# Three narrow products become one wide and one narrow; the work behind a feature-major job is moved and spread

## The reference, cut to what matters

```
# projection of the second block; xbc are 3072 of its 8224 columns
z, xbc, dt_raw, q, k, v = split(rmsnorm(h) @ w_in)
xbc = silu(causal_depthwise_conv(xbc, 4 taps) + conv_b)

# feed-forward part; w_up is 2048 x 11264, w_down 5632 x 2048
u = rmsnorm(h) @ w_up
u = causal_depthwise_conv(u, 3 taps) + ffn_conv_b
g_ff, u_ff = split(u)
h = h + (silu(g_ff) * u_ff) @ w_down
```

## Time and profile before

| | |
|---|---|
| median of three runs | 2368.04 us (2367.92 to 2368.23) |
| the profiled execution | 2368.59 us |
| its span, first to last instruction | 2366.8 us |
| instructions | 33302 |
| TensorE busy | 2253.2 us, 95% |
| VectorE busy | 1397.2 us, 59% |
| ScalarE busy | 989.5 us, 42% |
| mean granted TensorE clock | 0.981 |

### The profile page before, as it was taken

The page is one execution under the profiler, slowest core; times in us unless marked ns, Lnnn a source line. Parts: engine busy times, 40 slices in busy tenths (PEclk is TensorE's granted clock), DMA queues, the critical chain, the costliest instruction groups (busy, mean ns, idle before and its releaser), DMA issues.

```text
span 2366.8 us, 33302 instructions
## 1 busy us (share of the span) xinstructions
PE 2253.2 (95%) x13134; PEld 1927.9 (81%) x13134; DVE 1397.2 (59%) x1955; ACT 989.5 (42%) x1413; POOL 110.8 (5%) x106
## 2 busy tenths in 40 slices
PE   5899999998799899999989999999999999999998
PEld 1387888996568788998759888899999999788877
DVE  1357565634745577676566544667767776544465
ACT  1333232334544444444456544444444443344453
POOL 1000000002300021000000000000000000000000
PEclk8999999999899999999989999999999999999999
DMA  9975565543025466556400466556565665666554
GB/s 367 348 217 167 186 213 169 152 128 93 1 71 187 138 187 192 175 183 199 142 1 1 147 202 195 149 174 186 178 194 169 185 184 165 205 194 192 194 165 164
DMA packets 209084, 399.86 MB, mean 169 GB/s; under 512 B 15257, under 2 KB 23965, under 8 KB 208012
## 3 DMA queue, kind: packets, MB, share of 16 engines
q1 hardware_dynamic: 205520, 386.71, 51.9%
q0 software_dynamic: 2160, 7.20, 1.3%
q10 hardware_dynamic: 1292, 4.41, 0.5%
HBM read 395.25 MB, written 3.01 MB: 168 GB/s over the span
## 4 chain that ended last, share of the span: by engine, by line
PE 86%; DVE 6%; DMA 4%; ACT 2%; issue 1%; POOL 1%; SPq 0%; DVEq 0%; ACTq 0%
PE bank L1765 51%; PE bank L1776 27%; DMA ada_ring<-in_w_ada 4%; PE bank L1878 1%; PE bank L2046 1%; PE bank L1939 1%; PE bank L1861 1%; PE bank L1928 1%; PE bank L2059 1%; DVE wlo L1079 1%; PE bank L1870 0%; PE bank L1930 0%; POOL st L570 0%; PE bank L1905 0%; ACT kt L677 0%
## 5 line engine op out<-in xcount | busy, mean ns | idle before, releaser
L1079 DVE TENSOR_TENSOR wlo<-raw,whi 128x1024 fp32r<-128x1024 f32 (+2 forms) x649 | 773.5, 1204 | 584.7 <-ACT whi L670 570.3
L670 ACT ACTIVATE whi<-raw 128x1024 fp32r<-128x1024 f32 (+2 forms) x649 | 669.6, 1045 | 858.8 <-PE bank L1765 413.2
L1765 PE MATMUL bank<-whi,xl 128*128 128x512 f32 (+2 forms) x1904 | 734.0, 386 | 20.1 <-DVE wlo L1079 10.0
L1765 PE MATMUL bank<-whi,xh 128*128 128x512 f32 (+2 forms) x1904 | 728.4, 383 | 0.0
L1765 PE MATMUL bank<-wlo,xh 128*128 128x512 f32 (+2 forms) x1904 | 728.2, 382 | 0.0
L1776 PE MATMUL bank<-xl,whi 128*128 128x256 f32 x1792 | 507.9, 283 | 0.3 <-DVE xl L1128 0.3
L1776 PE MATMUL bank<-xh,wlo 128*128 128x256 f32 x1792 | 507.3, 283 | 0.0
L1776 PE MATMUL bank<-xh,whi 128*128 128x256 f32 x1792 | 507.2, 283 | 0.0
L1765 PEld LDWEIGHTS bank<-whi,xl 128*128 128x128 f32 x1904 | 359.1, 189 | 93.9 <-DVE wlo L1079 12.5
L1765 PEld LDWEIGHTS bank<-wlo,xh 128*128 128x128 f32 x1904 | 359.2, 189 | 68.7
L1765 PEld LDWEIGHTS bank<-whi,xh 128*128 128x128 f32 x1904 | 359.3, 189 | 65.7
(11 more groups left out here) (310 smaller groups left out, 1570.5 us busy)
## 6 DMA issues: line engine op xcount, KB each, us to landing
raw<-in_w_in SPq DMA_DIRECT2D x216, 512.0 KB, 4.4
raw<-in_w_up SPq DMA_DIRECT2D x176, 512.0 KB, 3.7
raw<-in_w_out SPq DMA_DIRECT2D x96, 512.0 KB, 4.6
raw<-in_w_down SPq DMA_DIRECT2D x88, 512.0 KB, 4.8
ada_ring<-in_w_ada SPq DMA_DIRECT2D x64, 512.0 KB, 11.6
gate_w<-in_w_ada SPq DMA_DIRECT2D x32, 512.0 KB, 3.9
raw<-in_w_ple_gate SPq DMA_DIRECT2D x32, 512.0 KB, 4.9
raw<-in_w_in SPq DMA_DIRECT2D x16, 384.0 KB, 3.3
```

The lines of the kernel that those rows point to most:

```text
L670: nc.scalar.activation(whi[:, slot, 0:size], raw[:, slot, 0:size], ACT.Copy).then_inc(hi_ready, 1)
L1079: tt_(wlo[:, slot, 0:size], raw[:, slot, 0:size], whi[:, slot, 0:size].bitcast(F32), ALU.subtract).then_inc(lo_ready, 1)
L1765: ins = mm(b4[tt][:, 0:width], x[:, o:o + P], w, start=k == 0 and i == 0, stop=k == last and i == 2)
```

## The change

`XH` and `XL` become the two halves of one tensor `XHL`. In `feature_major` a matmul of `whi` with 512 moving columns (256 of `XH`, then 256 of `XL`) and a matmul of `wlo` with the 256 columns of `XH` take the place of the three of 256 columns. The product is now in two halves of a bank, columns 0 to 255 (`whi` by `XH`) and 256 to 511 (the two others). So after each feature-major job ScalarE copies the upper half to SBUF and VectorE adds the lower half to it; only then are the banks free.

The taps then read SBUF. In the F jobs the first tap goes to ScalarE (slot 4), and VectorE has one tap a slot (5, 6, 7), tanh and silu follow in slots 9 and 10. In the `w_up` loop the copy and the addition come in slots 1 and 9, and all parts behind them one slot later. The last up job's parts are spread over the splits of the down tiles 2 to 8.

```diff
-        XH = at("xh", 12288, [P, 15360], FR)
-        XL = at("xl", 27648, [P, 15360], FR)
+        XHL = at("xhl", 12288, [P, 2, 15360], FR)
+        XH, XL = XHL[:, 0, :], XHL[:, 1, :]
+        UX = at("up_x", 51032, [P, 4, 256])
...
# TensorE, feature_major
-                        for i, (w, x) in enumerate(((whi, XL), (whi, XH), (wlo, XH))):
-                            ins = mm(b4[f][:, 0:256], w[:, slot, o:o + P], x[:, k * 256:(k + 1) * 256],
-                                     start=k == 0 and i == 0, stop=k == last and i == 2)
+                        mm(b4[f][:, :].rearrange("p (s n) -> p s n", s=2), whi[:, slot, o:o + P],
+                           XHL[:, :, k * 256:(k + 1) * 256], start=k == 0, stop=False)
+                        ins = mm(b4[f][:, 256:512], wlo[:, slot, o:o + P], XH[:, k * 256:(k + 1) * 256],
+                                 start=False, stop=k == last)
...
# ScalarE, F jobs
-                        ins = copy(XBC[:, (c - 2048) // P + i, :], b[i][:, 0:256])
-                    ins.then_inc(evac, 1)
+                        ins = copy(XBC[:, (c - 2048) // P + i, :], b[i][:, 256:512])
+                    ins.then_inc(low_copied, 1)
...
+                if kind == "F" and back == 4:
+                    act.wait_ge(evac, j + 1)
+                    if q >= 2:
+                        act.wait_ge(cv_used, q - 1)
+                    for i in range(4):
+                        k = 4 * q + i
+                        ins = nc.scalar.activation(CV[:, q % 2, i, :], XBC[:, k, :], ACT.Identity,
+                                                   scale=COLS[:, 200 + k:201 + k], bias=COLS[:, 80 + k:81 + k])
+                    ins.then_inc(tap0, 1)
-                if kind == "F" and back == 6:
+                if kind == "F" and back == 9:
...
# ScalarE, w_up jobs
+            def low_half(b4, used):
+                act.wait_ge(tile_used, used)
+                for f in range(4):
+                    ins = copy(UX[:, f, :], b4[f][:, 256:512])
+                ins.then_inc(low_copied, 1)
...
                 for k in range(16):
                     n = N_UP + 16 + k
                     hi(i * 16 + n, n % RING, 1024, i * 64 + 16 * (n // RING + 1))
-                    if k == 7:
+                    if k == 1:
+                        act.wait_ge(g_ready, i + 1)
+                        low_half(UB, i * 16 + (N_UP + 16))
+                    if k == 8:
                         act.wait_ge(ff_ready, i + 1)
...
+                    if k == 9:
+                        low_half(GB, i * 16 + (N_UP + 24))
-                    if k == 14:
+                    if k == 15:
...
-            for n in range(N_DN, N_DN + 4):
+            for n in range(N_DN, N_DN + 9):
                 split(n)
+                if n == N_DN + 1:
+                    low_half(UB, N_DN)
...
# VectorE, F jobs
-                if back in (3, 5):
...
+                if back == 3:
+                    dve.wait_ge(low_copied, q + 1)
+                    for i in range(4):
+                        x = XBC[:, 4 * q + i, :]
+                        ins = tt_(x, banks_of(j)[i][:, 0:256], x, ALU.add)
+                    own(ins)
+                    dve.sem_inc(evac, 1)
+                if back in (5, 6, 7):
+                    tap = back - 4
...
+                        ins = stt(y[:, tap:256], x[:, 0:256 - tap], wt, y[:, tap:256], ALU.mult, ALU.add)
...
# VectorE, w_up jobs
+            def whole(b4, count):
+                dve.wait_ge(low_copied, count)
+                for f in range(4):
+                    ins = tt_(UX[:, f, :], b4[f][:, 0:256], UX[:, f, :], ALU.add)
+                own(ins)
+                dve.sem_inc(evac, 1)
...
-                    if 1 <= k <= 6:
-                        after_up(i, i * 16 + (N_UP + 16), UB, k - 1)
+                    if 1 <= k <= 7:
+                        after_up(i, k - 2)
                     if k == 8:
                         low_product(i, i * 1024 + 4096)
-                    if 9 <= k <= 12:
-                        after_gate(i + 1, i * 16 + (N_UP + 24), GB, k - 9)
+                    if 9 <= k <= 13:
+                        after_gate(i + 1, k - 10)
             split(N_DN)
+            split(N_DN + 1)
+            after_up(10, -1)
             for part in range(6):
-                after_up(10, N_DN, UB, part)
-                if part in (1, 3, 4):
-                    split(N_DN + 1 + (1, 3, 4).index(part))
+                split(N_DN + 2 + part)
+                after_up(10, part)
+            split(N_DN + 8)
             low_product(10, 14336)
```

More of the change, by code:

```diff
@@ L677, in copy, with phase @@
                 return nc.scalar.activation(dst, src, ACT.Copy)
-            def phase(first, end, copy_out, later=None, moving=None):
-                for n in range(first + 2, end + 2):
+            def phase(first, end, copy_out, later=None, moving=None, begin=None):
+                for n in range(begin or first + 2, end + 2):
                     if moving is not None and n - 2 - first < len(ROUNDS[moving]):
@@ L1042, in later_dn @@
                     job_squares(J_DN, JUNK3)(j, back)
-            phase(N_DN + 2, N_PP, lambda j: None, later_dn)
+            phase(N_DN + 2, N_PP, lambda j: None, later_dn, begin=N_DN + 9)
             job_squares(J_DN, JUNK3)(J_DN + 3, 3)
@@ L1084, in split, with phase @@
                     lo(n, n % RING, TILES[n])
-            def phase(first, end, copy_out=None, later=None, moving=None):
-                for n in range(first + 2, end + 2):
+            def phase(first, end, copy_out=None, later=None, moving=None, begin=None):
+                for n in range(begin or first + 2, end + 2):
                     if moving is not None and n - 2 - first < len(ROUNDS[moving]):
@@ L1505, in later_in2 @@
                 q = (c - 2048) // W
-                if back in (3, 5):
[L1507 to L1520, removed]
+                if back == 3:
[7 more added lines that the diff above has]
+                    tap = back - 4
+                    if tap == 1:
+                        dve.wait_ge(tap0, q + 1)
+                    for i in range(4):
+                        k = 4 * q + i
+                        x, y = XBC[:, k, :], CV[:, q % 2, i, :]
+                        wt = COLS[:, 128 + (3 - tap) * 24 + k:129 + (3 - tap) * 24 + k]
+                        ins = stt(y[:, tap:256], x[:, 0:256 - tap], wt, y[:, tap:256], ALU.mult, ALU.add)
+                    if tap < 3:
+                        own(ins)
+                    else:
                         ins.then_inc(cv_ready, 1)
-                if back == 7:
+                if back == 10:
                     dve.wait_ge(cve_ready, q + 1)
@@ L1638, in _, with conv3 @@
             normalize(H, 40, 14, XN)
-            def conv3(b4, acc, chunk, part):
+            def whole(b4, count):
+                dve.wait_ge(low_copied, count)
+                for f in range(4):
+                    ins = tt_(UX[:, f, :], b4[f][:, 0:256], UX[:, f, :], ALU.add)
+                own(ins)
+                dve.sem_inc(evac, 1)
+            def conv3(acc, chunk, part):
                 def tap(k, i):
-                    x, y = b4[i][:, 0:256], acc[:, i, :]
+                    x, y = UX[:, i, :], acc[:, i, :]
                     wt = FC[:, bass.ds(chunk + ((2 - k) * 88 + i), 1)]
@@ L1658, in conv3, with after_up @@
                     own(tap(2, i + 1))
[L1660 to L1667, removed]
+            def after_up(pair, part):
+                if part == -1:
+                    whole(UB, 6 + 2 * pair + 2)
+                elif part < 4:
+                    conv3(AU, pair * 4 + 44, part)
                 if part == 4:
@@ L1678, in low_product, with after_gate @@
                     XH[:, sl].bitcast(F32).rearrange("p (c t) -> p c t", c=4), ALU.subtract).then_inc(ff_lo, 1)
[L1680 to L1684, removed]
+            def after_gate(pair, part):
+                if part == -1:
+                    whole(GB, 6 + 2 * pair + 1)
+                    return
+                conv3(AG, pair * 4, part)
                 if part == 3:
                     dve.sem_inc(g_ready, 1)
-                    dve.sem_inc(evac, 1)
             dve.wait_ge(s_fcc, 1)
@@ L1694, in _ @@
                 split(n)
-                if 9 <= n - N_UP <= 12:
-                    after_gate(0, N_UP + 8, GB, n - N_UP - 9)
+                if 9 <= n - N_UP <= 13:
+                    after_gate(0, n - N_UP - 10)
             with dve.Fori(0, 10) as i:
-                own.loop(i, 13)
+                own.loop(i, 15)
                 for k in range(16):
@@ L1718, in later_dn @@
                     one_round(R_PP, 0)
-            phase(N_DN + 2, N_PP, add_h(J_DN), later_dn)
+            phase(N_DN + 2, N_PP, add_h(J_DN), later_dn, begin=N_DN + 9)
             def later_pp(j, back):
```

8 lines of the change are left out of this document (7 added, 1 removed).

## The result

The changed kernel takes 2351.52 us (median of six runs, 2348.93 to 2352.20), the kernel before took 2367.98 beside it. The ratio is 0.9932, 95% interval 0.9921 to 0.9944: 16.5 us faster (13.3 to 18.7 by the interval), where 28.5 were forecast. The range ended at 2351, half a microsecond short.

The account below looks back on a forecast made before the run. The prediction took TensorE alone to set the pace. Products 23.9 us less and the start of the down projection 4.6 less, all else nothing, made 28.5 us less: 2339.5 us, range 2337 to 2351.

Parts of the forecast that it names:

- Part 1: Feature-major products: one wide and one narrow matmul take 346.7 ns for three narrow ones' 360.0, 1792 times: 23.9 us less.
- a line through three widths: TensorE's start distances at 256, 384 and 512 columns: columns / 2.4 GHz plus a fixed 13.3 ns.
- Rival B: Wide feature-major matmul pays the fixed part per piece, 240.0 ns; products gain nothing; 2363.5 us; chance 4%.
- Rival C: Feature-major products: only 2.5 of the 13.3 ns go with the instruction, the rest returns elsewhere; 2358.9 us; chance 3%.
- Part 2: Job boundary in `w_up`: the third tile's `lo` comes 0.56 us before it is needed, so no stall.
- Part 3: `w_up` loop: VectorE gains 34.6 us, to 81%, ScalarE 30.9, to 49%; both stay hidden behind TensorE.
- Part 4: F jobs: the copies, additions and moved taps cost nothing; 6 jobs x the lateness if wrong.
- Part 5: Start of the down projection: TensorE's three waits for `wlo` go, 4.6 us less.
- The signs it named: TensorE in `w_up`: starts 226.7 and 120 ns if right; wide at 240 or more, narrow over 120, or idle if wrong.
- rival A: Job boundary in `w_up` overruns, third tile late: 22 jobs stall by 0.5 us, 11 us; 2350.5 us; chance 7%.

Follow-up runs that it names:

- the run of addresses: Streams of wide and narrow matmuls alone, no kernel, reading the same or different blocks of weights: all thirteen kinds of pairs took 353.3 ns.
- the last kernel: Changed kernel with the whole first job of both stages in the order wide, wide, narrow, narrow, all others in turn: 2348.86 us, ratio 0.9924.

## Why the prediction was wrong

**The step that failed** is Part 1, "after, one wide and one narrow: 226.7 + 120.0 = 346.7 ns". Its addends were right for streams of one width: wide alone takes 226.7 ns and narrow alone 120.0. Adding them wasn't. I had drawn a line through three widths and read the 13.3 ns as a price of each matmul. Every row under that line was from a stream of one width. A stream of two widths has a length of its own, here 353.3 ns, which cost 12.0 of the 28.5 us.

- **Rival B** (the second piece is paid) came near in its first half, a wide start 240.0 ns before the next (236.5 on average, 241 for every third), and had the wrong cause: one piece took as long. It had the narrow one at 120.0 for 116.9 and so the pair at 360.0, where half of the gain did come.
- **Rival C** is the closest: "the rest returns elsewhere". It was put at 2358.9 us and had the loss in the width-free part of a matmul. The runs show a loss that hangs on the order and on what came before.
- **Part 2** (job boundary), **Part 3** (engine totals) and **Part 4** (F jobs) cost nothing, as forecast: no wait of TensorE in any of them, and three narrow matmuls with all the rest of the change took 2363.39 us. VectorE and ScalarE gained less than forecast (77 and 45% for 81 and 49%).
- **Part 5** (start of the down projection) came as forecast in the trace: 15.44 us became 10.89. In the times the spread alone gives 3.6 us of the 4.6, with an interval that holds both.
- **The signs it named.** The prediction named the right places to look, but its signs look at one matmul at a time. In the trace the two errors run against each other, and none of the signs fits: on average the wide one is off by 9.8 ns without reaching B's 240, and the narrow one stays below C's 120. The start of the next pair was the thing to measure. Part 1's own bounds for the extra cost, nothing to 13.3 ns, hold the measured 6.7. But it took nothing, gave the forecast's own range 0.4 ns of doubt, and counted the operand's two pieces as the only thing not shown. The other thing not shown was the alternation itself.
- **What was luck.** That 2351.52 us lies so near the end of the range says nothing for it: the range went to 2351 for rival A, a stall at the job boundary, and there was none.
- **Size.** With the stream in its fast rhythm a tile takes the forecast 2.773 us, and the kernel 2342.65 us for the forecast 2339.5; 0.9893 with its interval, on 2368.0, is 2339 to 2346.

**What stays open.** Why there are two rhythms. Pieces, banks, accumulation and the place of the weights don't explain it: both rhythms occur in the kernel, with two pieces, and in the streams with one piece, no accumulation and the same blocks of weights. Weight columns go with another loss, but behind one lead-in each. The form of the last group of two and two goes with the rhythm behind it in the kernels; what sets that form, and what does so for other lead-ins, isn't known. So whether a given order settles fast must be looked up in the trace of each build.

## What to carry to other kernels

A start distance read in a stream of equal matmuls is a price for that stream, not for a matmul; a mixed stream has to be measured. When matmuls of two widths take turns, compare their pair in the trace with the sum of the two alone, and if it is longer, reorder: two wide and two narrow took 348.3 ns a pair, within 0.3, in every stream and in the kernel where it was tried throughout, whatever ran ahead. When a stream is compared with another, put the same lead-in ahead of both. In this kernel the dense TensorE stage lost nothing to copies, additions and a second engine, because the one tile behind the boundary was in time, 1.3 us early; add up that one chain with all its handovers.

## What the runs showed of the hardware that was not expected

- The same dense stream of matmuls goes at 346.7 or at 353.3 ns a pair, at a granted clock of 1.00, by what ran ahead of it, and stays so for hundreds of pairs and over tile edges (1248 pairs at 353.3 ns in a row in the run of addresses, 320 at 346.7 in 40 tiles of the last kernel). Behind four matmuls of 128 columns, at the start of the `w_up` stage, it was slow although a tile of two and two stood ahead of them. In its slow form the starts follow a cycle of three pairs (236, 113, 233, 117, 241, 120 ns); in its fast form one of two pairs (233, 117, 231, 112 ns) or of one (230, 117 ns).
- A moving operand in two pieces 15360 floats apart costs nothing: 226.7 ns alone and 353.4 in a pair, as in one piece. Nor do four pieces of 128 columns: 226.7 ns.
- With 64 weight columns for 128, a narrow matmul takes 113.3 ns for 120.0, and a wide one 229.9 for 226.7. With 128 weight and 128 moving columns the distance is 111.7 ns, 58 more than the columns at 2.4 GHz, where it is 13.3 more at 256, 384 and 512.
